# Input projection of a two-block transformer: value columns computed token by token instead of strip by strip and turned

## The reference, cut to what matters

```python
h = modulate(rms_norm(x, attn_norm_w[i]), sh_a, sc_a)      # [1024 tokens, 1024]
proj = h @ w_in[i]
q_g, k_g, v_g, r_g, lr_f, lr_b, q_d, k_d, v_d = split_columns(proj, IN_SIZES)
```

## Time and profile before

| what | value |
|---|---|
| time, median of 3 runs | 2357.95 us (2350.28 to 2361.08) |
| span of the profiled execution | 2345.0 us |
| what the median has beyond that span | 12.95 us |
| TensorE busy | 2213.4 us, 94% of the span |
| VectorE, GpSimd, ScalarE busy | 65%, 34%, 32% |
| `projections` in the trace | first product 47.4 us, next stage from 355.96 us |
| value units 17 to 24 | 254.47 to 355.96 us |

### The profile page before, as it was taken

How to read it: one execution, slowest core, us unless ns; L and a number is a source line. 1 busy time by engine, 2 the same in 40 slices (tenths; PEclk the granted TensorE clock), 3 DMA queues, 4 the chain that set the end, 5 groups by cost and what they waited for, 6 DMA issues and landing times. The chain is left out here.

```text
span 2345.0 us, 28900 instructions
## 1 busy us (share of the span) xinstructions
PE 2213.4 (94%) x11384; PEld 1781.3 (76%) x11384; DVE 1527.6 (65%) x2201; ACT 754.6 (32%) x981; POOL 786.0 (34%) x517
## 2 busy tenths in 40 slices
PE   5999997899899999999999999898999899999998
PEld 2887786577777888888888887587887677777876
DVE  4774516798768888767677566634997544874344
ACT  4103412577323222222222233414223332443331
POOL 0222111210245666656656222211100011588720
PEclk8999999999999999999999999899999999999999
DMA  6595512332312343333333323236237532111132
GB/s 262 197 315 170 157 41 109 117 111 80 145 63 61 116 123 116 113 103 123 113 115 117 107 108 108 81 95 194 100 131 259 198 117 91 67 54 55 48 123 81
DMA packets 118673, 286.32 MB, mean 122 GB/s; under 512 B 11846, under 2 KB 57574, under 8 KB 115432
## 3 DMA queue, kind: packets, MB, share of 16 engines
q1 hardware_dynamic: 115540, 279.36, 35.3%
q10 hardware_dynamic: 3000, 5.15, 0.6%
HBM read 233.31 MB, written 67.93 MB: 128 GB/s over the span
## 5 line engine op out<-in xcount | busy, mean ns | idle before, releaser
L3346 POOL TENSOR_TENSOR w_lo<-w_staged,w_hi 128x1024 fp32r<-128x1024 f32 x66 | 162.0, 2455 | 348.7 <-ACT w_hi L3453 348.5
L276 POOL TENSOR_TENSOR w_lo<-w_staged,w_hi 128x1024 fp32r<-128x1024 f32 x26 | 63.7, 2450 | 375.1 <-ACT w_hi L226 375.0
L2137 POOL TENSOR_TENSOR w_lo<-w_staged,w_hi 128x1024 fp32r<-128x1024 f32 x23 | 58.3, 2534 | 273.2 <-ACT w_hi L2124 273.2
L2145 PE MATMUL ps_in<-h_hi,w_hi 128*128 128x512 f32 x400 | 126.5, 397 | 7.6 <-DVE h_lo L1435 3.6
L3453 ACT CAST w_hi<-w_staged 128x1024 fp32r<-128x1024 f32 x66 | 68.9, 1045 | 179.3 <-PE ps_dn L3373 178.7
L2145 PE MATMUL ps_in<-h_lo,w_hi 128*128 128x512 f32 x400 | 124.1, 391 | 0.0
L2145 PE MATMUL ps_in<-h_hi,w_lo 128*128 128x512 f32 x400 | 124.0, 391 | 0.0
L3198 DVE SCALAR_TENSOR_TENSOR ada_acc<-x_ctx,cond,ada_acc 128x512 f32<-128x512 f32 x112 | 119.7, 1099 | 2.0
L3364 PE MATMUL ps_up<-f_hi,w_hi 128*128 128x512 f32 x336 | 104.0, 391 | 4.2 <-POOL w_lo L3346 2.6
L3364 PE MATMUL ps_next<-f_hi,w_hi 128*128 128x512 f32 x336 | 107.2, 400 | 0.0
L3364 PE MATMUL ps_next<-f_lo,w_hi 128*128 128x512 f32 x336 | 103.7, 390 | 0.0
(11 more groups left out here) (665 smaller groups left out, 5931.0 us busy)
## 6 DMA issues: line engine op xcount, KB each, us to landing
w_staged<-in_w_ff SPq DMA_DIRECT2D x66, 512.0 KB, 3.7
x_ctx<-in_w_ada SPq DMA_DIRECT2D x48, 512.0 KB, 5.1
x_in<-in_w_ada SPq DMA_DIRECT2D x16, 1024.0 KB, 7.9
scratch_bias<-scratch_line SPq DMA_DIRECT2D x32, 512.0 KB, 7.7
att_bias<-scratch_bias SPq DMA_DIRECT2D x32, 512.0 KB, 3.2
w_staged<-in_w_in SPq DMA_DIRECT2D x17, 512.0 KB, 4.7
ada_w<-in_w_ada SPq DMA_DIRECT2D x8, 1024.0 KB, 19.5
scratch_x<-x SPq DMA_DIRECT2D x2, 4096.0 KB, 14.7
```

Source lines behind the costliest of these rows:

```text
L276: nc.gpsimd.tensor_tensor(st.lo[i % 2][:, 0:widths[i]], st.staged[i % 2][:, 0:widths[i]], st.hi[i % 2][:, 0:widths[i]].bitcast(F32), ALU.s ...
L2137: nc.gpsimd.tensor_tensor(st.lo[i % 2][:, :], st.staged[i % 2][:, :], st.hi[i % 2][:, :].bitcast(F32), ALU.subtract).then_inc(st.split, 1)
L2145: last = nc.tensor.matmul(ps[i % 2][:, a:a + BANK], u[i % 2][:, k * P:(k + 1) * P], r[:, k, a:a + BANK], start=(k == 0 and part == 0), sto ...
L3346: nc.gpsimd.tensor_tensor(st.lo[i % 2][:, :], st.staged[i % 2][:, :], st.hi[i % 2][:, :].bitcast(F32), ALU.subtract).then_inc(st.split, 1)
```

## The change

The value columns are computed in the other orientation: a block of `h` for 128 tokens is the stationary operand, and the weights of four value strips, 512 columns, are streamed. The result stands with tokens on the partitions and needs no turn. It is made in four passes: two halves of the columns (the GLA values, the attention values) by two groups of four token tiles. A pass has four units; a unit holds two of the eight blocks of the width for four strips, and makes 24 products (`tile_products`). The four tiles of a pass take the four banks of `ps_in0` and `ps_in1`; they are copied to `x_in` when the pass is over, by ScalarE in the first three passes, by ScalarE and VectorE in the last. There are 33 units instead of 25. The weights of each half are loaded and split once for each group of tokens, so twice. The last gate round, `turn_k` of rounds 2 and 3 and `gate_z` of round 3 are threaded into the new, shorter units.

```diff
-    UNITS = [("w_in", j) for j in ORDER] + [("w_v", i) for i in range(2 * HEADS)]
+    PASSES = [(half, group) for half in range(2) for group in range(2)]
+    PER_PASS = KD // 2
+    TILES = TT // 2
+    UNITS = [("w_in", j) for j in ORDER] + [("w_v", half * PER_PASS + u) for half, _ in PASSES for u in range(PER_PASS)]
...
+        def v_unit(p, u):
+            return N_IN + PER_PASS * p + u
+
+        def v_place(t):
+            return ps[1 - t // 2][:, t % 2 * BANK:(t % 2 + 1) * BANK]
+
+        def v_out(p, t):
+            half, group = PASSES[p]
+            return x_in[:, TILES * group + t, half * BANK:(half + 1) * BANK]
+
+        def wait_tile(engine, p, t):
+            if t < TILES - 1:
+                engine.wait_ge(v_done, (TILES - 1) * p + t + 1)
+            else:
+                engine.wait_ge(st.done, base + v_unit(p, PER_PASS - 1) + 1)
...
             for i, (name, j) in enumerate(UNITS):
                 if i >= READY:
                     sp.wait_ge(st.split, base + i - 1)
-                    sp.dma_start(st.staged[i % 2][:, :], g.dram[name][j]).then_inc(st.loaded[i % 2], 16)
+                    if name == "w_v":
+                        half, u = divmod(j, PER_PASS)
+                        sp.dma_start(st.staged[i % 2][:, :].rearrange("p (s n) -> p s n", s=HEADS),
+                                     g.dram[name][HEADS * half:HEADS * half + HEADS, :, 2 * P * u:2 * P * u + 2 * P].rearrange("s p n -> p s n")
+                                     ).then_inc(st.loaded[i % 2], 16)
...
-            def take_out(j):
-                act.wait_ge(st.done, base + N_IN + j + 1)
-                if j == 1:
-                    act.wait_ge(chained, 3 * len(ROUNDS))
-                if j >= 2:
-                    act.wait_ge(turned, j - 1)
-                nc.scalar.copy(vT[j % 2], ps[(N_IN + j) % 2][:, :]).then_inc(v_taken, 1)
+            def take_tiles(p, tiles):
+                for t in tiles:
+                    wait_tile(act, p, t)
+                    nc.scalar.copy(v_out(p, t), v_place(t)).then_inc(v_taken, 1)
...
-                if i - 1 in ROUNDS:
+                if i - 1 in ROUNDS and i <= N_IN:
                     first_half(SLOTS_OF.index(i - 1), *ROUNDS[i - 1])
-                if i - 2 in ROUNDS:
+                if i - 2 in ROUNDS and i <= N_IN + 1:
                     second_half(SLOTS_OF.index(i - 2), *ROUNDS[i - 2])
-                if i > N_IN:
-                    take_out(i - 1 - N_IN)
-            take_out(2 * HEADS - 1)
+                if i == v_unit(0, 2):
+                    first_half(LAST, *ROUNDS[SLOTS_OF[LAST]])
+                if i == v_unit(0, 3):
+                    second_half(LAST, *ROUNDS[SLOTS_OF[LAST]])
+                for p in range(len(PASSES) - 1):
+                    if i == v_unit(p + 1, 0):
+                        take_tiles(p, range(TILES))
+            take_tiles(len(PASSES) - 1, range(0, TILES, 2))
...
+            def tile_products(p, u, kk):
+                i, k, group = v_unit(p, u), 2 * u + kk, PASSES[p][1]
+                for t in range(TILES):
+                    at = (TILES * group + t) * P
+                    if k == 0:
+                        if p:
+                            pe.wait_ge(v_taken, TILES * (p - 1) + t + 1)
+                        else:
+                            pe.wait_ge(placed, N_IN - 1 + t // 2)
+                    for part, (h, v) in enumerate(((hi, st.hi), (hi, st.lo), (lo, st.hi))):
+                        last = nc.tensor.matmul(v_place(t), h[:, k, at:at + P], v[i % 2][:, :].rearrange("p (s k n) -> p k s n", s=HEADS, k=2)[:, kk],
+                                                start=(k == 0 and part == 0), stop=(k == KD - 1 and part == 2))
+                    if k == KD - 1 and t < TILES - 1:
+                        last.then_inc(v_done, 1)
+                if kk == 1:
+                    last.then_inc(st.done, 1)
...
-            for i in range(2, n):
+            for i in range(2, N_IN):
                 pe.wait_ge(st.split, base + i + 1)
-                if i < N_IN + 2:
-                    pe.wait_ge(placed, i - 1)
-                else:
-                    pe.wait_ge(v_taken, i - 1 - N_IN)
+                pe.wait_ge(placed, i - 1)
...
-                if i > N_IN:
-                    turn_tiles(i - 1 - N_IN)
-            turn_tiles(2 * HEADS - 1)
+            for p in range(len(PASSES)):
+                for u in range(PER_PASS):
+                    pe.wait_ge(st.split, base + v_unit(p, u) + 1)
+                    tile_products(p, u, 0)
+                    if (p, u) == (0, 2):
+                        turn_k(LAST - 1)
+                    if (p, u) == (1, 2):
+                        turn_k(LAST)
+                    tile_products(p, u, 1)
+                    if (p, u) == (0, 0):
+                        gate_z(LAST, *ROUNDS[SLOTS_OF[LAST]])
...
-            for i in range(n):
+            for i in range(N_IN + 3):
                 if i < N_IN:
                     place_strip(i)
-                elif i > N_IN:
-                    j = i - 1 - N_IN
-                    dve.wait_ge(turned, j + 1)
-                    nc.vector.tensor_copy(vtok[:, :, j, :], ps_v[:, :, :]).then_inc(stored, 1)
...
-            dve.wait_ge(turned, 2 * HEADS)
-            nc.vector.tensor_copy(vtok[:, :, 2 * HEADS - 1, :], ps_v[:, :, :]).then_inc(stored, 1)
+            for t in range(1, TILES, 2):
+                wait_tile(dve, len(PASSES) - 1, t)
+                nc.vector.tensor_copy(v_out(len(PASSES) - 1, t), v_place(t)).then_inc(stored, 1)
```

More of the change, by code:

```diff
@@ L2007, in projections @@
     OWN = 5
-    UNITS = [("w_in", j) for j in ORDER] + [("w_v", i) for i in range(2 * HEADS)]
+    PASSES = [(half, group) for half in range(2) for group in range(2)]
+    PER_PASS = KD // 2
+    TILES = TT // 2
+    UNITS = [("w_in", j) for j in ORDER] + [("w_v", half * PER_PASS + u) for half, _ in PASSES for u in range(PER_PASS)]
     ROUNDS = {12: (0, 0), 14: (0, 1), 16: (1, 0), 18: (1, 1)}
     SLOTS_OF = tuple(ROUNDS)
+    LAST = len(ROUNDS) - 1
     READY = 2
@@ L2021, in projections @@
     z, nab, cs, kst = (mixed[:, s, :] for s in range(4))
-    vT = [mixed[:, 4 + s, :] for s in range(2)]
-    scan_mask = vT[1]
+    scan_mask = mixed[:, 5, :]
     lr, place = mixed[:, 6, :], [kst_tok[1], mixed[:, 7, :]]
@@ L2039, in projections @@
         spilled = [g.early(f"in_spilled{s}") for s in range(2)]
+        v_done = g.early("v_done")
         v_taken = g.early("v_taken")
-        turned = g.early("v_turned")
         stored = g.early("v_stored")
@@ L2070, in _ @@
                     sp.wait_ge(st.split, base + i - 1)
-                    sp.dma_start(st.staged[i % 2][:, :], g.dram[name][j]).then_inc(st.loaded[i % 2], 16)
+                    if name == "w_v":
[4 more added lines that the diff above has]
+                    else:
+                        sp.dma_start(st.staged[i % 2][:, :], g.dram[name][j]).then_inc(st.loaded[i % 2], 16)
                 if i == 2:
```

## The result

The changed kernel takes 2371.35 us, median of 7 runs (2364.82 to 2376.59), beside 2357.95 us for the kernel before (7 runs). The ratio is 1.0063, 95% interval 1.0048 to 1.0078: 14.9 us more, 11.3 to 18.4 (the two medians are 13.4 apart). I forecast 2369 us, in a range from 2360 to 2378, as "within 0.5%" with 0.53 and "slower" with 0.44. The size and the mechanism were right. The measured ratio lies on the other side of the bound of 0.5%; the interval of the first series still reaches across it (0.48%), that of e9 does not (0.53%).

The account below looks back on a forecast made before the run. TensorE was taken as the bound of the value stretch. Turns and tail -9.4, the wait for strip 16 with its clock +8.4 and unit 21's late start +11.9 gave +11.0 on 2357.95: 2369 us, range 2360 to 2378.

Parts of the forecast that it names:

- What bounds it, and what goes: Value stretch: TensorE alone sets the end; six turns between units (5.5 us) and 3.9 at the tail go, 9.4 removed.
- Pause 1: Inside unit 17, TensorE waits 5.96 us from 255.83 until VectorE has copied strip 16.
- The clock behind it: After the wait for strip 16, TensorE runs at half clock for a while, losing 2.4 us (2.1 to 2.8).
- Pause 2 and the last gate round: Before unit 20, TensorE waits about 7 us; gate round 3 holds the casts, so unit 21 starts at 299.6, 11.9 late.
- Unit 21 to the end: Units 21 to 32 at 5.44 us each, one turn of 0.92 and a tail of 1.2, ending at 367.0.
- the fall behind pause 3: Rival: clock falls again after the 2.1 to 2.9 us wait before unit 21, total +13.5, 2371.5 us; 20%.
- What I cost at nothing: Value units: doubled loads, casts and subtractions, and the streamed operand in four runs of 128, add 0 us.
- The time: Whole kernel: the stretch's 11.0 us added to the median 2357.95, giving 2369 us, 0.47% more.
- Clock kept at pause 1: Rival: the clock stays up after the wait for strip 16, total +8.6, 2366.5 us; 8%.
- Products of the new form slower: Rival: the value products each take longer, crossing 0.5% from 0.003 us each, at most 2436 us; 4%.
- weights late: Rival: value weight loads take 9 us instead of 4, costing 2 us per pair of units, 2381 us; 6%.
- pauses hidden: Rival: strip 16 is copied early and the gate round does not hold the casts, -9.4, 2348.5 us; 5%.

Follow-up runs that it names:

- e9: The changed kernel, unaltered, timed again on one chip: ratio 1.0071 (1.0053 to 1.0090) against the kernel before.
- e3: Changed kernel with strip 16 copied early, and the turn of round 2 and the casts of units 20 to 22 moved ahead: 2348.54 us, ratio 0.9983.
- e5: Kernel before with only one transpose of eight in each turn of values, output not the reference's: 2352.81 us, ratio 0.9996.
- e1: Changed kernel with VectorE copying strip 16 before the scan of gate round 2: 2362.74 us, ratio 1.0045.
- e8: The changed kernel, unaltered, run once more for its profile: stretch 112.5 us.
- e2: Changed kernel with the turn of round 2 one unit earlier and the casts of units 20 to 22 ahead of gate round 3's parts: 2353.70 us, ratio 1.0009.
- e7: Changed kernel with GpSimd's subtraction of unit 20 held back until VectorE is through gate round 3: 2364.98 us, single run.
- e4: Changed kernel with 12, 14 and 9 unused products of 128x256 put into TensorE's three pauses: 2360.64 us, ratio 1.0039.

## Why the prediction was right, by its steps

- **What bounds it, and what goes.** Right. Turns and tail were to give 9.4; e3 without pauses is 8.8 below, e5 confirms the price of a turn (6.1 where 6.4 was expected). The tail is 1.2 us (the last product starts at 366.00, with 0.227 it is 366.23, and the next stage begins at 367.41), with a copy of 0.69 where I took 0.7.
- **Pause 1.** Forecast 5.96, shown 5.66, at the place and by the copy named (L2246, which is L2285 in the changed kernel). e1 removes it and wins 6.5.
- **The clock behind it.** Forecast 2.4, between 2.1 and 2.8. Shown: 2.05 in the first profile; in e8 the clock was back at 266.0, 5.3 us after 260.64, so 2.7. Over five executions with a pause 1 of 5.65 or 5.66 it came back after 4.1, 5.3, 5.8 (e9), 3.5 (e2) and 3.4 us (e7), half of that lost, 1.7 to 2.9: my two ends stood a little too close together.
- **Pause 2 and the last gate round.** From `store_k(2)` to L2293 5.85 (5.86), from there to the end of L2303 6.83 (6.8), pause before unit 20 6.61 (7), from `store_k(2)` to unit 21 298.33 - 278.57 = 19.8 (20.0). e2 shows the queue as the cause and e7 what the subtraction costs inside it. That unit 20's own start doesn't matter held too: in e7 it starts at 291.14 instead of 287.90, and the stretch is not longer (112.3). The rule of the Trainium skill (SBUF — State Buffer, Who interferes with whom), that one of these two engines blocks the other for a whole instruction, agrees with 4.31 beside 2.29. I had the scan free and L2264 held up as in the earlier trace rows, and it was the scan; that the price came out the same was luck.
- **Unit 21 to the end.** 69.1 where 67.4 was forecast: nearly all of it the 1.6 of the fall behind pause 3, which I had as a rival with 20%. Without it, in e8 and e9, the same part takes 67.5. The forecast's stretch of 112.5 was thus met in e8 and e9, and in the first profile two misses met: unit 21 began 0.6 us earlier than forecast, counted from the first value product, and the rest took 1.7 longer. Pause 3 was 2.52, 2.26 and 2.15 in the three profiles, and the clock fell behind the first alone; in e1 it was 2.65, and the clock fell. With the 2.62 that left it alone in the earlier trace rows, the border "near 3 us" that I drew is not there: the clock fell behind two shorter pauses, and between 2.5 and 2.7 us it went either way. It is worth 1 us of the stretch on balance (113.6 against 112.5 and 112.7).
- **What I cost at nothing.** Right within 0.5 us. From 303 to 367 TensorE is busy 63.39 of 64 us; loads land in 3.2 to 7.1 us, median 3.4, where I had 3.4 to 4.3 and room for 7. (The 3.9 us from a unit's end to the next weights add up to 3.8; the 1.6 to spare go with the 3.8.)
- **The time.** The stretch was forecast 11.0 longer; three profiles have 12.1, 11.0 and 11.2. The time is 14.9 above, in e9 16.7. What carried it clear of the 0.5%, 11.8 us, is mainly the excess outside the stretch, 2.8 to 5.5 us, which no step of mine had: I added the stretch's 11.0 to the median and took everything outside as unchanged, without a row for it. e5, with the old orientation, shows that time and stretch part by such an amount even there. The 12.95 us between median and span, which I named beside it, are no term of the forecast, as they stand on both sides of the comparison; but all of them beyond some 2 us are a difference between executions, more than ten times the 0.8 us of room under the bound that I argued about.
- **The other rivals.** Clock kept at pause 1: fell in all profiles of the changed kernel. Products of the new form slower, weights late, pauses hidden: shown wrong by e3 and by the pauses themselves.

## What to carry to other kernels

A unit of work that is cut in half leaves everything that was threaded beside it twice as large: before halving, list what each helper engine does in one unit's time and in which order, for a cast queued behind a long chain is late even if the engine is idle most of the time. A result that needs all banks at once inherits the wait of the slowest bank; look at who frees it and what that engine does just then. The gain was real, 8.8 us of the stretch, and showed once one copy, one turn and three casts were moved ahead (e3: 4 to 7 us of the time).

## What the runs showed of the hardware beyond what I expected

- The clock fell behind pauses of 2.52 us and 2.65 us (e1), and not behind 2.26, 2.15 or the earlier trace rows's 2.62: near that length the same program loses it in one execution and keeps it in another. After pauses of 5.65 and 5.66 us it was back 3.4 to 5.8 us after the products went on. Products without use in the pauses kept it at 1.00 throughout (e4).
- A scan of 2.29 us on VectorE took 4.31 and, in round 2 of e1, 4.41 behind a subtraction on GpSimd that had begun just before it, while the subtraction kept its 2.4.
- The new streamed operand, four runs of 128 elements 256 apart, costs what one run of 512 does (0.2266): the 15 products from 362.82 to 366.00 start 0.227 us apart (3.18 by 14).
